# A decoder layer on one core: later side loads, norm spreads in rounded products, a reordered softmax loop, other fillers before the last projection, and an end shared by three engines

## The reference, cut to what matters

```
mod = silu(c) @ w_ada + b_ada               # six vectors of 1024 for each sequence
h   = RMSNorm(x) * (1 + scale1) + shift1
u   = h @ w_in                              # q, k, v, indexer, conv input, branch gates
A   = attention over the keys that an indexer picks; q and k are normed by head
B   = silu(LayerNorm(causal_conv(glu(u)))) @ w_conv_out
x   = x + gate1 * ((sig(gA) * (A @ w_o_attn) + sig(gB) * B) @ w_out)
h2  = RMSNorm(x) * (1 + scale2) + shift2
x   = x + gate2 * PEER(h2)                  # 16384 experts, 16 picked for each of 8 heads
```

## Time and profile before

| | us |
|---|---|
| timed runs, median (lowest to highest) | 1246.91 (1246.56 to 1247.79) |
| the profiled execution, own time | 1244.62 |
| its span, first to last instruction | 1242.8 |
| PE busy | 1205.0 |
| DVE busy | 921.6 |
| POOL busy | 612.3 |
| ACT busy | 593.2 |

### The profile page before, as it was taken

The page is one execution under the profiler, slowest core; times in us unless marked ns, Lnnn a source line. Parts: engine busy times, 40 slices in busy tenths (PEclk is TensorE's granted clock), DMA queues, the critical chain, the costliest instruction groups (busy, mean ns, idle before and its releaser), DMA issues.

```text
span 1242.8 us, 28224 instructions
## 1 busy us (share of the span) xinstructions
PE 1205.0 (97%) x8845; PEld 1113.0 (90%) x8845; DVE 921.6 (74%) x2255; ACT 593.2 (48%) x1016; POOL 612.3 (49%) x307
## 2 busy tenths in 40 slices
PE   5999999989999999999999999999999999999997
PEld 3888887989979999999999999999888888888886
DVE  4899956966756999859999998000567888888866
ACT  2433444666434445445455555444455555555552
POOL 0565564603746577766666666777203444444100
PEclk9999999999999999999999999999999999999999
DMA  9986564424633456655555555667767898888763
GB/s 356 332 285 203 178 216 179 145 81 154 236 134 130 154 188 207 211 191 183 180 184 179 188 178 184 207 215 240 263 224 292 305 335 308 307 305 307 272 227 125
DMA packets 113995, 273.12 MB, mean 220 GB/s; under 512 B 30928, under 2 KB 54192, under 8 KB 113552
## 3 DMA queue, kind: packets, MB, share of 16 engines
q1 hardware_dynamic: 105920, 248.96, 58.7%
q0 software_dynamic: 6432, 19.71, 4.5%
q10 hardware_dynamic: 1584, 3.68, 0.8%
HBM read 249.30 MB, written 23.00 MB: 219 GB/s over the span
## 4 chain that ended last, share of the span: by engine, by line
PE 88%; SPq 3%; issue 2%; DMA 2%; DVE 2%; POOL 2%; ACT 1%; DVEq 0%; ACTq 0%; POOLq 0%
PE ps L2241 19%; PE ps L2184 11%; PE ps L2191 11%; PE ps L2185 11%; PE ps L2244 10%; PE ps L1845 6%; PE ps L1861 6%; PE ps L1855 6%; PE ps L2220 2%; DMA ring<-in_stream 2%; SPq L562 2%; POOL split L672 1%; PE ps L1949 1%; SPq L556 1%; PE ps L1877 1%
## 5 line engine op out<-in xcount | busy, mean ns | idle before, releaser
L732 POOL TENSOR_TENSOR split<-ring,split 128x1024 fp32r<-128x1024 f32 x128 | 307.6, 2404 | 138.4 <-ACT split L1013 138.4
L1013 ACT ACTIVATE split<-ring 128x1024 fp32r<-128x1024 f32 x256 | 271.6, 1061 | 174.6 <-PE ps L2241 167.9
L672 POOL TENSOR_TENSOR split<-ring,split 128x1024 fp32r<-128x1024 f32 x77 | 188.1, 2446 | 189.8 <-ACT split L832 188.3
L2184 PE MATMUL ps<-h2r,split 128*128 128x288 f32 x1024 | 278.6, 297 | 0.7 <-ACT big L1039 0.5
L2185 PE MATMUL ps<-h2r,split 128*128 128x288 f32 x1024 | 278.8, 296 | 0.0
L2241 PE MATMUL ps<-h2r,split 128*128 128x512 f32 x1024 | 257.4, 392 | 1.4 <-DVE h2r L1691 1.4
L2241 PEld LDWEIGHTS ps<-h2r,split 128*128 128x128 f32 x1024 | 184.2, 189 | 34.5 <-ACT act L1069 1.6
L2184 PEld LDWEIGHTS ps<-h2r,split 128*128 128x128 f32 x1024 | 193.0, 188 | 1.2 <-ACT big L1039 0.8
L2185 PEld LDWEIGHTS ps<-h2r,split 128*128 128x128 f32 x1024 | 192.4, 188 | 0.0
L2191 PE MATMUL ps<-h2r,split 128*128 128x288 f32 x1024 | 156.6, 295 | 0.1
L1697 DVE TENSOR_TENSOR split<-ring,split 128x1024 fp32r<-128x1024 f32 x128 | 156.0, 1219 | 0.0
(11 more groups left out here) (290 smaller groups left out, 1613.9 us busy)
## 6 DMA issues: line engine op xcount, KB each, us to landing
ring<-in_stream SPq DMA_DIRECT2D x371, 512.0 KB, 3.4
act_dram<-act SPq DMA_DIRECT2D x128, 128.0 KB, 1.7
big<-in_stream SPq DMA_DIRECT2D x20, 512.0 KB, 7.9
parts<-act_dram SPq DMA_DIRECT2D x16, 512.0 KB, 4.7
big<-act_dram SPq DMA_DIRECT2D x16, 512.0 KB, 5.3
big<-in_cache_k SPq DMA_DIRECT2D x16, 128.0 KB, 2.7
big<-in_cache_v SPq DMA_DIRECT2D x16, 128.0 KB, 3.3
s_act_dram<-act SPq DMA_DIRECT2D x128, 16.0 KB, 1.5
```

The source lines that it names most:

```text
L672: nc.gpsimd.tensor_tensor(split[:, n % 2, 1], ring[:, POS[CUT[n]] % R, :], split[:, n % 2, 0].bitcast(f32), ALU.subtract).then_inc(lin_lo, 1)
L732: nc.gpsimd.tensor_tensor(split[:, (n + ODD) % 2, 1], ring[:, slot_of(n), :], split[:, (n + ODD) % 2, 0].bitcast(f32), ALU.subtract).then_ ...
L1013: nc.scalar.activation(split[:, (n + ODD) % 2, 0], ring[:, slot_of(n), :], ACT.Copy).then_inc(hi_ready, 1)
L2184: MM(out, u_hi[:, k], h_hi[:, k], start=(k == 0), stop=False)
```

## The change

It has six parts.

1. **Later loads.** POOL issues `v_w`, `dist` and `causal` after its fourth low part; ACT issues `stateT` and `qkg` after the sigmoid of `conv_g` 1; the pages at positions 20, 22 and 23 go to 44, 46 and 47.
2. **Norm spreads.** Each of the ten is two fp32r products (high and low part of the rows) in place of one fp32 product; one step later in the loop. ACT and DVE make the parts once, DVE a rounded copy of the identity.
3. **Softmax loop.** The reciprocal comes before the `conv_out` work; the sample stages come one or two steps later; the sample tokens' low part of `attn` goes behind the loop.
4. **Fillers.** `late_ada` runs as two unbroken groups with 2 fillers between them, in place of 16 fillers in pairs and the second group within `peer_q` 0; there now stand 8 single fillers.
5. **First value weights apart.** They lie in `hot1`, so they are made before the last score is done; PE starts the outputs with banks 2 to 7.
6. **The end.** ACT takes the second half of banks 1, 3 and 5 out, POOL adds it and does the sample tokens; SP stores in five pieces.

```diff
-QK_AT = 3
+QK_AT = 4
-PAGE_AT = [pos for pos in range(NFIRST * R + R, NRING) if pos - R + 1 not in ADA_AT][:NSEQ * NPAGES]
+PAGE_AT = [pos for pos in range(NFIRST * R + 2 * R, NRING) if pos - R + 1 not in ADA_AT][:NSEQ * NPAGES]
...
+        wr_first = hot1[:, 0:2].rearrange("p n a i -> p (n a i)").rearrange("p (a t) -> p a t", a=2)
...
+            for k in range(0, KC, 2):
+                sp.wait_ge(y_out, sum(n not in SHARED for n in range(k + 2)))
+                sp.wait_ge(y_odd, sum(n < k + 2 for n in SHARED))
+                if k == KC - 2:
+                    sp.wait_ge(s_scaled, 2)
+                    sp.dma_start(a["yT"][:, :, TP:T], ye[:, :, TP:T]).then_inc(stored, 16)
+                sp.dma_start(a["yT"][:, k:k + 2, 0:TP], ye[:, k:k + 2, 0:TP]).then_inc(stored, 16)
...
             for n in range(NHEAD - 2):
                 low_tile(n)
+                if n == 3:
+                    pool.dma_start(v_w, a["v_w"]).then_inc(vw_in, 16)
+                    for dst, src in ((dist_w, "dist"), (causal_w, "causal")):
+                        pool.dma_start(dst, a[src]).then_inc(mask_in, 16)
...
+            for i, k in enumerate(SHARED):          # POOL; SHARED = (1, 3, 5)
+                pool.wait_ge(y_scaled, i + 1)
+                pool.wait_ge(y_half, k + 1)
+                nc.gpsimd.tensor_tensor(ye[:, k, 0:TP], ye[:, k, 0:TP], y_low[:, i], ALU.add).then_inc(y_odd, 1)
...
+                    if m == 1:                       # ACT, conv_g
+                        for dst, src in ((staged_s, "stateT"), (qkg, "qkg")):
+                            eng.dma_start(dst, a[src]).then_inc(conv_in, 16)
...
+                if n == 1:                           # ACT, indexer loop
+                    eng.wait_ge(qk_rstd, 1)
+                    nc.scalar.activation(qk_parts[0:len(QK), 0], qk_rms[0:len(QK)], ACT.Copy).then_inc(qk_high, 1)
...
+            turn(NSUB // R - 1, False, lambda: high_weights(0, 0, 0, True), R - 2)
...
+            for i, k in enumerate(SHARED):          # ACT, the end
+                eng.wait_ge(bank_done, k + 1)
+                nc.scalar.activation(y_low[:, i], ps[k][:, TP:2 * TP], ACT.Copy, scale=gate2[:, k, 0:1]).then_inc(y_scaled, 1)
...
                 if n + 1 < NQ * H:                   # DVE, softmax loop
                     bias(n + 1)
+                dve.wait_ge(exped, n + 1)
+                V.reciprocal(stat[:, n, 2:3], stat[:, n, 1:2]).then_inc(inverse, 1)
                 if n % 2:
...
-                dve.wait_ge(exped, n + 1)
-                V.reciprocal(stat[:, n, 2:3], stat[:, n, 1:2]).then_inc(inverse, 1)
...
-                if n in (1, 3):
+                if n in (1, 4):
...
+            second_half(0)                           # DVE, the end
+            for k in SHARED:
+                dve.wait_ge(y_scaled, SHARED.index(k) + 1)
+                first_half(k)
+                first_half(k + 1)
+                if k + 2 == KC - 1:
+                    first_half(KC - 1)
+                second_half(k + 1)
+            second_half(KC - 1)
...
-                    MM(pa[2 + m % 2][:, 0:T], ident[0:len(QK), m:m + 1].to_broadcast([len(QK), P]), qk_rms[0:len(QK)],
-                       start=True, stop=True).then_inc(qk_spread, 1)
+                    place = qk_place[0:len(QK), m:m + 1].to_broadcast([len(QK), P])
+                    for part in range(2):
+                        last = MM(pa[2 + m % 2][:, 0:T], place, qk_parts[0:len(QK), part], start=(part == 0), stop=(part == 1))
+                    last.then_inc(qk_spread, 1)
...
-            for s in range(R):
-                for j in range(2):
-                    late_ada(0, s, j)
+            for i in range(2):
+                for s in range(R):
+                    for j in range(2):
+                        late_ada(i, s, j)
+                if i == 0:
                     keep_busy(2)
...
-                for k in range(KC):
+                for k in (*range(2, KC), 0, 1) if first else range(KC):
+                    if first and k == 0:
+                        pe.wait_ge(gelued, NSUB)
                     ins = high(k)
```

More of the change, by code:

```diff
@@ L640, in _ @@
                 v_turn(g2 * 2 + 2, 1)
[L642 to L647, removed]
+            for k in range(0, KC, 2):
[5 more added lines that the diff above has]
+                sp.dma_start(a["yT"][:, k:k + 2, 0:TP], ye[:, k:k + 2, 0:TP]).then_inc(stored, 16)
+            sp.wait_ge(stored, 16 * 9)
         @block.gpsimd
@@ L1059, in _, with turn @@
                 gelu(c, c, c < 2)
-            def turn(g, tokens4, behind_first=None):
+            def turn(g, tokens4, behind=None, at=0):
                 for n in range(R):
@@ L1069, in turn @@
                     nc.scalar.activation(act[:, n % 2], ps[n % 2][:, 0:T], ACT.Gelu_apprx_tanh).then_inc(gelued, 1)
-                    if behind_first and n == 0:
-                        behind_first()
+                    if behind and n == at:
+                        behind()
                     if tokens4:
@@ L1687, in weights, with low @@
                                 ALU.mult).then_inc(weighted, 1)
-            def low(c, b, n):
+            def low(c, b, n, first=False):
                 dve.wait_ge(w_hi, c + 1)
-                V.tensor_tensor(wr[:, n % 2, 1], act_bs[b][:, n], wr[:, n % 2, 0].bitcast(f32), ALU.subtract)\
-                    .then_inc(w_lo, 1)
+                both = wr_first if first else wr[:, n % 2]
+                V.tensor_tensor(both[:, 1], act_bs[b][:, n], both[:, 0].bitcast(f32), ALU.subtract).then_inc(w_lo, 1)
             def value_low(c, n, used, value):
@@ L1722, in v_turns @@
                         weights(g2, 0, 0)
-                    low(c, b, n)
+                    low(c, b, n, first and i == 0)
                     slot = adds.index(i) if sparse is not None and i in adds else None
@@ L1730, in v_turns @@
                         weights(g2 + 1, 0, 0)
-                    value_low(c, n, *((u_done, NSUB - 1 + i) if first and i < 2 else (o_done, c - 1)))
+                    value_low(c, n, *((u_done, NSUB) if first and i < 2 else (o_done, c - 1)))
                     if slot is not None:
@@ L1825, in _, with keep_busy, linear_cut @@
             g_hi, g_lo = (rhs_other[:, part].rearrange("p (k t) -> p k t", t=T) for part in range(2))
-            def linear_cut(key, *halves, between=None):
+            def keep_busy(n):
+                for _ in range(n):
+                    MM(pa[3][:, 0:T], g_lo[:, 0, 0:P], g_lo[:, 0], start=True, stop=True)
+            def linear_cut(key, *halves):
                 n = CUT.index(key)
@@ L2129, in _ @@
                 linear_cut(("out", n))
-            def keep_busy(n):
-                for _ in range(n):
-                    MM(pa[3][:, 0:T], g_lo[:, 0, 0:P], g_lo[:, 0], start=True, stop=True)
             keep_busy(6)
@@ L2146, in _ @@
             for n in range(2 * PH):
-                linear_cut(("peer_q", n), between=(lambda k: late_ada(1, k // 2, k % 2)) if n == 0 else None)
+                linear_cut(("peer_q", n))
                 if n == 1:
@@ L2236, in outputs @@
                 v = [split[:, (n + ODD) % 2, part].rearrange("p (k m) -> p k m", m=P) for part in range(2)]
-                w_both = wr[:, n % 2].rearrange("p a t -> p (a t)")
+                w = wr_first if first else wr[:, n % 2]
+                w_both = w.rearrange("p a t -> p (a t)")
                 def high(k):
```

106 lines of the change are left out of this document (59 added, 47 removed).

## The result

The changed kernel is slower by 0.22%: 1248.22 us (median of 22 runs, 1243.67 to 1254.46) against 1245.57 (22 runs, 1242.41 to 1247.79), ratio 1.0022 [1.0013, 1.0031], +2.7 us where -5.2 was forecast. The profiled execution has a span of 1247.0, 4.2 above that of before.

A forecast was written before the change was run, and what follows sets the result against it. PE, busy for 1205.0 of 1242.8 us, was taken as the bound. The terms +1.0 - 2.5 + 0.3 - 2.6 - 1.4 + 0 gave -5.2, so 1241.7 us on the median; range 1236.0 to 1247.5.

The forecast's parts named there:

- Part 1: Later loads, PE from 38 to 109 us: 3.1 us won early, some 4.1 lost later; net +1.0 (-3.1 to +6.4).
- of 6.4 us some 4.1 lost: Moved loads, from about 46 us: 6.4 us of DMA time, 2.3 us free in the next 18, so 4.1 lost.
- rival C: Moved loads starve the ring at 50 to 64 us and PE's clock falls: +9.9 there, 1250.6 us in all; chance 0.12.
- Part 2: Norm spreads in the indexer loop: 3.1 us less work, 0.6 only lengthening PE's wait for DVE; -2.5 (-3.1 to 0).
- Part 3: Softmax loop: the gap at 253.61 moves, the merge_conv wait grows 0.6, a later gap shrinks; +0.3 (-1.5 to +1.5).
- Part 4: Fillers around peer_q 0: ada groups run unbroken and peer_q 1 starts earlier; -2.6 us (-3.0 to +1.0).
- Rival D: The clock falls at peer_q 0, making the fillers' term +1.0, the sum -1.6 and the time 1245.3 us; chance 0.08.
- Part 5: First value weights at the start of the outputs: the 1.35 us gap at 876.67 goes; -1.4 (-1.5 to -0.8).
- If the next ring loads were late: Start of the outputs: ring loads waiting for the last store of scores, if late, would take back 0.6 us.
- Part 6: The kernel's end: DVE finishes earlier, but SP's stores leave the last byte as late as now; 0 (-1.5 to +1.5).
- the last byte is as late as now: Kernel's end: 1.3 us for the samples' store and 0.65 per 256 KB piece, so no gain.
- a new fall of the clock shows: The prediction's sign of being wrong; the other was 38 to 126 us moving by over 4 us either way.

The follow-up runs named there:

- part 2 alone: The kernel before with only the norm spreads changed to two fp32r products each: ratio 0.9995, -0.6 us.
- no1: The changed kernel with the later loads undone, all five other parts kept: ratio 0.9995 to the kernel before, -0.6 us.
- c245: The kernel before with norm spreads, fillers and first value weights changed: ratio 0.9966, -4.2 us.
- c245b: The kernel before with norm spreads, fillers and first value weights changed, plus ten unread products before the loop's last sums: ratio 0.9963, -4.6 us.
- c2345b: The kernel before with norm spreads, softmax loop, fillers and first value weights changed, plus ten unread products before the last sums: ratio 0.9974, -3.2 us.
- part 5 alone: The kernel before with only the first value weights apart and banks 2 to 7 first: ratio 0.9991, -1.1 us.
- c2345: The kernel before with norm spreads, softmax loop, fillers and first value weights changed: ratio 0.9990, -1.2 us.
- parts 1 and 2 alone: Two kernels, each the kernel before with one part: only the later loads, ratio 1.0032 (+4.0 us); only the norm spreads, ratio 0.9995 (-0.6 us).
- the pages alone: The kernel before with only the pages loaded later, the side loads where they were: ratio 0.9999.

## Why the prediction was wrong, step by step

The parts alone come to +1.6 where -5.2 was forecast. Of these 6.8 us, part 1 is 3.0, part 2 is 1.9 and part 6 is 1.9; parts 3, 4 and 5 miss by 0.5 or less each. The last 1.1, up to +2.7, are in no part alone.

- **Part 1** was taken at +1.0 and is +4.0. The first half of its working was right: some 3 us come back ahead of the moved loads (2.8 measured). The step that failed is "of 6.4 us some 4.1 lost, since 13% of the next 18 us (2.3 us) are free". It priced DMA time alone and put the clock at nothing. Measured in the same stretch are 3.0 us without a fall and 6.2 with one: a wait of 2 to 3 us lets the clock fall in most executions. That mechanism, a starved ring and a fall behind it, stood in the prediction as rival C with 0.12. C's 3.5 for a fall was near (2.7, with 1.1 of longer waits beside it); its 6.4 with nothing won ahead of it was not.
- **Part 2** was taken at -2.5 and is -0.6. A spread is 0.36 us in two products, not 0.27, and ACT's copy is not hidden: PE waits 0.64 at the second step. That leaves -1.3 at the last sums. The wait there grew as forecast (1.37 to 1.81), but what the clock does behind it was in no term: in the profiles of part 2 alone and of the kernel after, its earlier and longer fall takes 1.5 back.
- **Part 3**: +0.3 was right alone (+0.5, unclear); that its waits can bring a fall, as in two of five profiles, was not in the sum.
- **Part 4**: -2.6, in the profile -2.55 and in the times -3.1; no fall. Rival D did not come.
- **Part 5**: -1.4, in the profile -1.59 and then +0.43, in the times -1.1. "If the next ring loads were late" is what happened in five of seven profiles with part 5 in which these loads stood behind the wait: 0.38 to 1.50 us at the fourth or fifth tile in no1, c245, c245b, c2345b and the changed kernel, none with part 5 alone and in c2345.
- **Part 6** was taken at 0 and is +1.7 in the profile, +1.9 in the times. The last store is issued 3.1 us behind the start of PE's last product, as forecast, and the last byte is through 5.5 us behind that start, where it was 5.7 before. The step that failed is the one from there to the end, "the last byte is as late as now" taken as a gain of 0: the span ends 2.8 us behind the last byte and not 0.9, 5.2 and not 3.2 behind the last issue, and 6.42 behind POOL's last instruction. I followed DVE, SP and the bytes; that POOL's own end can set the end of the span was in no term.
- **223 to 247**: +1.21 from DVE and POOL at one another was in no term. It shows in four other profiles as well (24.75 or 24.78 us: parts 1 and 2 alone, the pages alone, parts 2, 4 and 5), and is a matter of 0.3 us of phase.

The prediction's own signs spoke too: it called itself wrong if a new fall of the clock shows, and two show in the profile where there were waits, at 64 and at 268 us, beside one at 26.

## What to carry to other kernels

Where PE sits at 97%, price a wait by what the clock does behind it: with the moved loads one execution of seven lost next to nothing, and the other six took 3.7 to 5.4 us more. It follows, though it was not tried here, that moved transfers belong in a stretch whose DMA share is low for as long as the consumers' buffer lasts. And before a last piece of work goes to an engine that had been finished for long, look at how far the span's end lies behind that engine's last instruction.

## What was not expected of the hardware

- The span ends 6.41 to 6.48 us behind POOL's last instruction in four kernels, whatever the stores; with two shared banks it is 6.75, and the end no later than before. In the kernel before, DVE's last instruction ends 3.2 us before the end.
- The clock also falls, in some executions only, at 25 to 35 us in ten of twenty profiles (seven of them of kernels that have the early loads of before) and at 330 to 340 in two. A wait makes a fall likely and not certain.
- Two DVE operations of 128x128 with two SBUF inputs took 3.47 in place of 0.63 us beside a POOL operation that had started 0.03 us earlier.
- SP issued its next ring loads 4.5 to 5.9 us after the last 16 KB store of 128-byte pieces, in eight profiles. With part 5, the two shortest (4.5 and 4.6) are those without a wait at the output tiles.
